# Second layer's MLP in two phases with down rows gated on GpSimd, and another order of loads at the start of the down phase

## The reference, cut to what matters

```python
def modulate(h, shift, scale):
    return layer_norm(h) * (1.0 + scale) + shift

def post_norm_residual(h, y, gate, g, b):
    return layer_norm_affine(DEEPNORM_ALPHA * h + gate * y, g, b)

def sq_relu_mlp(u, w1, w2):
    return jnp.square(jax.nn.relu(u @ w1)) @ w2
...
for i in range(DEPTH):                                  # DEPTH = 2; mlp0, mlp1
...
    h = post_norm_residual(h, sq_relu_mlp(modulate(h, sh2, sc2), mlp_w1[i], mlp_w2[i]), g2, ln_g[i, 1], ln_b[i, 1])
...
h = h + jnp.square(jax.nn.relu(_rmsnorm(h, mlp_norm_g[l]) @ w_up[l])) @ w_down[l]   # mlp2
```

## Time and profile before

| | us |
|---|---|
| three runs | 3166.06, 3170.08, 3171.18 |
| median | 3170.08 |
| the profiled execution | 3174.14 |
| its span, first to last instruction | 3172.4 |
| PE busy in it | 3061.9 |
| mean granted TensorE clock | 0.992 of full |

### The profile page before, as it was taken

The page is one execution under the profiler, slowest core; times in us unless marked ns, Lnnn a source line. Parts: engine busy times, 40 slices in busy tenths (PEclk is TensorE's granted clock), DMA queues, the critical chain, the costliest instruction groups (busy, mean ns, idle before and its releaser), DMA issues.

```text
span 3172.4 us, 36169 instructions
## 1 busy us (share of the span) xinstructions
PE 3061.9 (97%) x14331; PEld 2511.8 (79%) x14331; DVE 2130.2 (67%) x2769; ACT 1344.0 (42%) x2002; POOL 822.5 (26%) x543
## 2 busy tenths in 40 slices
PE   7999999999999999989999999999998999999998
PEld 2888888778888888868788888888777778887887
DVE  4716598577677777586766555666797676667576
ACT  4411387363333333442633333334427465553334
POOL 0010335155433443221444444314000212120000
PEclk9999999999999999999999999999999999999999
DMA  7426322212322332111111111121111225456533
GB/s 236 145 88 209 89 67 59 102 38 93 106 95 98 100 102 82 49 43 53 35 52 54 54 54 47 53 67 41 40 54 54 93 97 177 148 197 226 188 109 120
DMA packets 202163, 302.83 MB, mean 95 GB/s; under 512 B 12135, under 2 KB 137690, under 8 KB 201994
## 3 DMA queue, kind: packets, MB, share of 16 engines
q1 hardware_dynamic: 174906, 206.46, 20.7%
q0 software_dynamic: 18736, 63.65, 5.3%
q10 hardware_dynamic: 8352, 30.41, 2.7%
HBM read 251.19 MB, written 49.28 MB: 95 GB/s over the span
## 4 chain that ended last, share of the span: by engine, by line
PE 77%; DVE 12%; ACT 6%; issue 2%; DMA 2%; POOL 1%; SPq 0%; DVEq 0%; ACTq 0%; POOLq 0%
PE psum L669 24%; PE psum L671 23%; PE psum L670 23%; DVE page_r L680 2%; PE psum L1399 2%; DVE dw L4161 2%; DVE small L819 1%; ACT temp L1004 1%; ACT page_r L675 1%; ACT U_hi L675 1%; DVE U_lo L680 1%; DMA page<-in_ada_w_dram 1%; DVE H L1679 1%; PE psum L1374 1%; PE psum L865 1%
## 5 line engine op out<-in xcount | busy, mean ns | idle before, releaser
L669 PE MATMUL psum<-U_hi,page_r 128*128 128x512 f32 x1884 | 743.4, 395 | 24.6 <-DVE U_lo L680 9.7
L671 PE MATMUL psum<-U_hi,page_r 128*128 128x512 f32 x1884 | 734.7, 390 | 0.0
L670 PE MATMUL psum<-U_lo,page_r 128*128 128x512 f32 x1884 | 734.6, 390 | 0.0
L680 DVE TENSOR_TENSOR page_r<-page,page_r 128x1024 fp32r<-128x1024 f32 (+1 forms) x208 | 294.7, 1422 | 284.9 <-ACT page_r L675 276.2
L669 PE MATMUL psum<-page_r,act_page_r 128*128 128x512 f32 x1232 | 480.4, 390 | 5.6 <-DVE page_r L680 5.6
L670 PE MATMUL psum<-page_r,act_page_r 128*128 128x512 f32 x1232 | 480.1, 390 | 0.0
L669 PEld LDWEIGHTS psum<-U_hi,page_r 128*128 128x128 f32 x1884 | 354.3, 188 | 113.5 <-DVE U_lo L680 19.6
L671 PE MATMUL psum<-page_r,act_page_r 128*128 128x512 f32 x1120 | 436.4, 390 | 0.0
L675 ACT CAST page_r<-page 128x1024 fp32r<-128x1024 f32 (+1 forms) x271 | 276.3, 1024 | 324.5 <-DMA page<-in_mlp_w_dram 92.7
L671 PEld LDWEIGHTS psum<-U_hi,page_r 128*128 128x128 f32 x1884 | 354.2, 188 | 75.0
L670 PEld LDWEIGHTS psum<-U_lo,page_r 128*128 128x128 f32 x1884 | 354.6, 188 | 70.2
(11 more groups left out here) (394 smaller groups left out, 4809.8 us busy)
## 6 DMA issues: line engine op xcount, KB each, us to landing
page<-in_mlp_w_dram SPq DMA_DIRECT2D x128, 512.0 KB, 4.2
act_page<-d_act_mlp SPq DMA_DIRECT2D x56, 512.0 KB, 3.6
d_act_mlp<-page POOLq DMA_DIRECT2D x111, 256.0 KB, 5.8
page<-in_ada_w_dram SPq DMA_DIRECT2D x48, 512.0 KB, 4.7
page<-in_w_in_dram SPq DMA_DIRECT2D x38, 512.0 KB, 4.0
pair_raw<-in_w_up_dram SPq DMA_DIRECT2D x14, 1024.0 KB, 6.2
ada_land<-in_ada_w_dram ACTq DMA_DIRECT2D x24, 512.0 KB, 4.7
even_raw<-in_w_down_dram SPq DMA_DIRECT2D x8, 1024.0 KB, 6.2
```

Source lines behind the costliest of these rows:

```text
L669: pe.matmul(out, l_hi, r_hi, start=start, stop=False, skip_group_check=read_between)
L670: pe.matmul(out, l_hi, r_lo, start=False, stop=False, skip_group_check=read_between)
L671: return pe.matmul(out, l_lo, r_hi, start=False, stop=stop, skip_group_check=read_between)
L680: return dve.tensor_tensor(lo, src, hi.bitcast(F32), ALU.subtract).then_inc(*k.lo.inc(*key))
```

## The change

The second layer's MLP uses the two-phase functions too. What is new in them for it:

- POOL multiplies the down rows by the gate, 32 instructions of 128x2x512 (`pool_gate_rows`), in the order: two for product 1 before the last but one pair's spills, two more after the last pair's first spills, the rest behind all spills. ACT and DVE wait for the gated rows (`wait_rows`) where they waited for the loads.
- The first add of each quarter also multiplies H by ALPHA (one instruction as before).
- The boundary to the next stage is worked into the last two products: at step d of product 12 the post norm of tile d (measure, root, scale, normed tile; POOL's two operations follow), from (12, 2) on ACT's sums of squares for the pre-norm; the transposes of tiles 0 to 3 stand inside the last product on PE, between its second and third token tile, on four banks. Tiles 4 to 7 follow the last product's adds.
- The weight of the last step has a place of its own; other page slots and the loads of the next stage's weights move accordingly.

For both two-phase MLPs SP issues `acts(2)` and `acts(3)` ahead of `odds(0, 0)`.

```diff
-TWO_PHASE = ("mlp2",)
+TWO_PHASE = ("mlp1", "mlp2")
+GATE_OF = {"mlp1": (1, 1)}
...
+            if after and t == 1:
+                pe_turn_chunk(k, pe, on, after.name, 0, [after.place(k, e) for e in range(TPC)],
+                              lambda e: on.wait_ge(*after.hat(k, e)), slots=CHAIN_BANKS)
...
+def wait_rows(k, on, name, p, s, d):
+    if name in GATE_OF:
+        on.wait_ge(*k.pool_gated.at(name, p, s, d))
+    else:
+        on.wait_ge(*(k.odd_in if p in ("2", "3") else k.even_in)[d].at(name, s))
+
+def pool_gate_rows(k, pool, on, name, p, s, d):
+    rows = down_source(k, p, d)
+    cols = CH if p in ("7", "3") else 0
+    on.wait_ge(*k.gate_ok.at(*GATE_OF[name]))
+    on.wait_ge(*(k.odd_in if p in ("2", "3") else k.even_in)[d].at(name, s))
+    pool.tensor_tensor(rows, rows, k.row_gate[:, cols:cols + CH].unsqueeze(1).to_broadcast([P, 2, CH]), ALU.mult).then_inc(
+        *k.pool_gated.inc(name, p, s, d))
...
     if g == DOWN_STEPS - 1:
-        on.wait_ge(*k.lo.at("weight", name, g - 3))
+        on.wait_ge(*k.up_done.at(name, "4", PAIRS - 1))
...
         if p == "57":
-            on.wait_ge(*k.odd_in[e].at(name, s))
+            wait_rows(k, on, name, "7", s, e)
+            wait_rows(k, on, name, "3", s, e)
...
+def act_behind_step(k, act, on, b, i, d):
+    if i == FIRST_DONE + 1:
+        act_root(k, act, on, P, b.name, "post", d)
+        act_normed(k, act, on, b, d)
+    t = STEPS_OF * (i - FIRST_DONE - 1) + d - 2
+    if 0 <= t < TPC:
+        act_pre_square(k, act, on, b, t)
+
+def dve_behind_step(k, dve, on, b, i, d):
+    if i == FIRST_DONE + 1:
+        dve_norm_measure(k, dve, on, b, "post", d)
+        dve_norm_scale(k, dve, on, b, "post", d)
+        k.smalls.take(on, (b.name, "pre", d))
+    t = STEPS_OF * (i - FIRST_DONE - 1) + d - 3
+    if 0 <= t < TPC:
+        dve_norm_scale(k, dve, on, b, "pre", t)
...
+    gate("1", 0, 2)
+    gate("1", 0, 3)
     for what in ("12",) + sums:
         store(what, PAIRS - 1)
+    for d in range(STEPS_OF):
+        gate("7", 0, d)
+        gate("3", 0, d)
+    for d in range(STEPS_OF):
+        gate("2", 0, d)
+    for d in range(STEPS_OF):
+        gate("1", 1, d)
+        gate("7", 1, d)
+    for p in ("3", "2"):
+        for d in range(STEPS_OF):
+            gate(p, 1, d)
...
-    odds(0, 0)
     acts(2)
     acts(3)
+    odds(0, 0)
     odds(0, 1)
...
-    pe_mlp(k, pe, on, "mlp1", BOUNDARY[2], BOUNDARY[3])
+    pe_two_phase(k, pe, on, "mlp1", BOUNDARY[2], BOUNDARY[3])
```

More of the change, by code:

```diff
@@ L981, in dve_start, with pe_turn_chunk @@
         dve_weights(k, dve, on, s)
-def pe_turn_chunk(k, pe, on, stage, c, src, ready, groups=range(KT)):
+def pe_turn_chunk(k, pe, on, stage, c, src, ready, groups=range(KT), slots=(None,)):
     for i in groups:
-        b = k.banks.take(on, ("turn", stage, c, i), (k.taken, ("turn", stage, c, i)))
+        b = k.banks.take(on, ("turn", stage, c, i), (k.taken, ("turn", stage, c, i)), slot=slots[i % len(slots)])
         for t in range(TPC):
@@ L1015, in dve_turn_chunk @@
             between(i)
-STASHED = {"pre4": "mlp2"}
+STASHED = {"post2": "mlp1", "pre4": "mlp2"}
 def stash_of(k, c, i):
@@ L1785, in __init__, with behind @@
         self.on_pool = TT - 2 if from_u else TT - 1
+    @property
+    def behind(self):
+        return self.down[0] if self.down[0] in TWO_PHASE else None
     def by_pool(self, tt):
@@ L1818, in place_free @@
             on.wait_ge(*k.down_done.at(self.down, TT - 1, 1))
+        elif self.behind and tt < TPC:
+            on.wait_ge(*k.lo.at("weight", self.behind, STEPS_OF * (FIRST_DONE + 1) - 1))
+        elif self.behind and tt < TT - 2:
+            on.wait_ge(*k.up_done.at(self.behind, "4", PAIRS - 1))
+        elif self.behind:
+            on.wait_ge(*k.down_done.at(self.down, TT - 1, 1))
         elif not self.from_u:
@@ L1830, in u_free @@
             on.wait_ge(*k.down_done.at(self.down, TPC - 1 if c == 0 else TT - 1, 1))
+        elif self.behind and c == 0:
+            on.wait_ge(*k.lo.at("weight", self.behind, STEPS_OF * FIRST_DONE - 1))
+            on.wait_ge(*k.folded.at(self.behind, "down", 1, "6", STEPS_OF - 1))
+        elif self.behind:
+            on.wait_ge(*k.up_done.at(self.behind, "4", PAIRS - 1))
         else:
@@ L3010, in act_down_weight @@
     if p in ("1", "2", "3"):
[L3011 removed]
+        wait_rows(k, on, name, p, s, d)
     else:
@@ L3067, in dve_down_add, with act_pre_square, act_two_phase @@
         on.wait_ge(*k.h_back[tt].at(name))
-    dve.tensor_tensor(h, h, k.bank(name, "down", i, t), ALU.add).then_inc(*k.h_added.inc(name, i, t))
-    if DOWN_ORDER[i] in ("4", "2"):
+    if name in GATE_OF and not earlier:
+        m = dve.scalar_tensor_tensor(h, h, ALPHA, k.bank(name, "down", i, t), ALU.mult, ALU.add)
+    else:
+        m = dve.tensor_tensor(h, h, k.bank(name, "down", i, t), ALU.add)
+    m.then_inc(*k.h_added.inc(name, i, t))
+    if i >= len(PRODUCTS) and DOWN_ORDER[i] in ("4", "2"):
         k.h_added.also(name, tt)
+        k.h_added.also((name, BLOCKS - 1), tt, 1)
 FIRST_DONE = len(DOWN_ORDER) - 3
-def act_two_phase(k, act, on, name, before):
+def act_pre_square(k, act, on, b, t):
+    s = k.small[:, k.smalls.of(b.name, "pre", t), :]
+    on.wait_ge(*b.gained(k, t))
+    on.wait_ge(*k.act_done.now())
+    act.activation(k.ada_land[:], k.H[:, t, :], ACT.Square, scale=D ** -0.5, accum_out=s[:, 13:14]).then_inc(
+        *k.act_done.inc("pre", b.name, t))
+    on.wait_ge(*k.act_done.now())
+    act.activation(s[:, 14:15], s[:, 13:14], ACT.Sqrt, bias=k.eps[:, 0:1]).then_inc(*k.rooted.inc(b.name, "pre", t))
+def act_behind_step(k, act, on, b, i, d):
[13 more added lines that the diff above has]
+        dve_norm_scale(k, dve, on, b, "pre", t)
+def act_two_phase(k, act, on, name, before, after=None):
     row = lambda p, *part: act_row_sum(k, act, on, name, p, before, *part)
@@ L3092, in act_two_phase @@
             op("1", PLAIN + 1)
-        act_plain_tile(k, act, on, name, i, c)
+        if not (before.rows and (i, c) in UP_AHEAD):
+            act_plain_tile(k, act, on, name, i, c)
         if (i, c) == (FB - 1, 0):
```

91 lines of the change are left out of this document (64 added, 27 removed).

## The result

The changed kernel takes 3196.39 us (median of four, 3194.46 to 3197.54), the kernel before 3170.36 in the same comparison: 1.0082 of it, 95% interval 1.0069 to 1.0094. It is 26 us slower; 3174 was forecast, with a range from 3134 to 3188.

A forecast was written before the change was run, and what follows sets the result against it. PE's instruction count was taken to set the time, other engines mattering only where PE waits. Terms -43.4 - 3.6 - 4 + 23.2 + 6.4 + 22.2 + 3 gave +3.8 us, forecast 3174 us, range 3134 to 3188.

The forecast's parts named there:

- matmuls and old waits gone: mlp1: 192 fewer matmuls at 0.226 us, -43.4 us, and three waits of the merged last block gone, -3.6 us.
- start of the down phase: mlp1: 12 POOL gates behind the last spill alternate with DVE, so PE waits; +21 us, +2.2 for the lower clock.
- second half's gates: mlp1's down phase: 16 POOL gates beside DVE, partly absorbed; +6.4 us, ends 0 and 13, full alternation 8.
- product 12: mlp1: the norm's DVE-ACT chain and POOL's two operations per tile lengthen four steps; +20 us, full alternation 22.5.
- transposes: mlp1's last product: PE waits 1.6 to 4.4 us for ACT with four banks free; taken as +3 us.
- moved loads: mlp2's down phase: activations come about 2.8 us earlier, shortening the 5.61 us wait; -4 us, ends -1.5 to -7.8.
- the lower clock: mlp1: slower matmuls charged at 2.2 us each, behind the down phase start's longest wait and in product 12.
- (b): Rival, mlp1: DVE and POOL fully alternate wherever POOL has work; 3182 us, up to 3188; chance 0.22.
- (a): Rival, mlp1: gates slip into DVE's gaps; -31 us, or -29 with a clock drop, giving 3141; chance 0.28.
- Four fifths of the way: mlp1: share taken from gates in gaps (5 us) towards full alternation (25) at the down phase's start; also in product 12.
- PE's busy time should fall by 43 us: Sign, whole kernel: PE's busy time must fall by about 43 us.
- The other sign: mlp1: the prediction is wrong if the added waits are under 35 us or over 60.

The follow-up runs named there:

- e8: The changed kernel with 24 of the 32 gates done by DVE just ahead of the sums that read the rows; 3164.86 us, ratio 0.9982.
- e2: The changed kernel with POOL's two norm operations for tiles 0 to 3 at mlp1's end on 8 of 1024 columns; 3182.31 us, ratio 1.0035.
- e5: The changed kernel with the last product's eight groups of transposes spread behind its second, third and fourth token tiles; 3195.34 us, ratio 1.0081.
- e1: The changed kernel with each POOL gate on 2x8 of its 2x512 columns, same instructions, waits and loads; 3158.45 us, ratio 0.9961.
- e9: The changed kernel with each tile's norm in product 12 spread over two steps; 3188.42 us, ratio 1.0050.
- e12: The changed kernel with the edits of e8, e9 and e5, and DVE also doing the four gates of product 1's first half; 3156.63 us, ratio 0.9955.
- e4: The kernel before with only mlp2's loads moved, third and fourth step's activations ahead of the first odd rows; 3168.04 us, ratio 0.9993.
- e6: The changed kernel with the old order of loads, first odd rows ahead of those activations, in both two-phase MLPs; 3196.97 us, ratio 1.0086.

## Why the prediction was wrong, point by point

"Lower clock" is the time that is left when the waits and the matmuls at 0.2267 us each (the distance of two starts at full clock, a step is 5.44 us) are taken off a stretch between two rows.

| step of the sum | forecast | measured |
|---|---|---|
| matmuls and old waits gone | -47.0 | -47.1 (by count) |
| mlp1's up phase: new waits, old ones gone, lower clock | 0 | +6.6, -2.1, +1.9 |
| start of the down phase (to step 6), with lower clock | +23.2 | +25.0 |
| second half's gates, with lower clock | +6.4 | +13.5 |
| product 12 | +20 | +20.4 |
| last product: transposes, with lower clock | +5.2 | +8.9 |
| moved loads in mlp2 and all else behind mlp1 | -4 | -1.6 |
| ahead of mlp1 (scatter) | 0 | -3.3 |
| sum | +3.8 | +22.2 (span +22.3) |

(The 5.2 are the 3 for the transposes and the 2.2 for the clock behind product 12.)

The mechanism, DVE and POOL alternating on a shared port, was right; the terms were too small. Three failed. The second half's gates, taken at +6.4, cost 13.5. The up phase of mlp1 stood at nothing, with no reason given, and cost 6.4. And the lower clock was charged behind two waits, 4.4 us, while it followed on nearly all: where no later wait took it up, about 13 us.

- **Matmuls**: right. PE's busy time fell by 20 us less than by count; the lower clock, at which matmuls take longer, accounts for it. In the down phase, from 1853.9 to 2230.7, 1344 matmuls and the transposes are worth 308.9 us and the waits 48.8; 19 of the 376.8 us are left for the lower clock. I had put in 4.4. It followed on nearly all waits of over 2 us, down to one of 2.40 us (from 1973.87 to 2058.92 are 14 steps of 5.44, the wait of 6.55, and 2.3 more). The earlier trace rows had shown it behind a wait of 5.61. But not all of the 19 us came on top: some 8 of them, in product 12 and behind the first wait of the down phase, lie between waits for engines that set the round, where PE would have waited longer at the full clock (see e8). That leaves about 11 in the down phase, and 1.9 in the up phase.
- **Start of the down phase**: right in size (25 by full alternation, 21 + 2.2 taken, 25.0 measured, of which waits are 20.7), wrong in its shape in the profiled execution: I had the first wait at the fourth step, and POOL's long hold of the port brought it to the third. In e2 and e5 the waits are 4.9, 5.9 and 5.8 and 4.8, 4.7 and 6.2 us, before the third, fourth and fifth step, where I had 10, 8.5 and 5.5 before the fourth, fifth and sixth; with the lower clock e2's start costs some 23 us. That the whole came out near is in part luck. e1 shows the cause: without the gates' time 4.1 us are left, against the 5 that I gave to loads alone. e8 shows that it is POOL's hold and not the multiplication.
- **Second half's gates**: the mechanism was right (e1: both waits gone), the size too small: 13.5 against 6.4, my upper end of 13 nearly to the point. I had taken four fifths of full alternation's 8; here the waits are the full price, 8.95, and the lower clock behind them, which I had put at nothing, is 4.6 on top.
- **Product 12**: right, 20.4 against 20; a round takes 10.35 us where full alternation would give 10.8. The 20.4 are 14.3 of waits and 6.1 of lower clock; as the other engines set the round, it is their sum that the 20 stood for, and the four fifths that gave it had no row behind them: the hit is in part luck. e2 and e9 show both parts of it, POOL's operations (11.3 us of e2's gain lie in product 12; its start was some 2.4 better) and the chain between DVE and ACT.
- **Transposes**: the waits between groups are 4.6 us, beyond my 4.4, and the clock adds 4.3.
- **What was not in the sum**: the up phase. The 3.75 us come from ACT, busy with the sums of rows when PE wants a bank; mlp2 had no such wait in the trace of before, and I expected none in mlp1 either. The 1.65 and 1.23 are two early gates beside DVE; I had said that they only come before the last spills (e1: both gone; e12: one gone, one 0.76). Small waits of 4.4 us at mlp1's start stood in the trace of before, where I had read none; 2.1 of them went. **Moved loads**: -1.4 us of wait in mlp2, -2.7 in e4, near the smaller of my ends, and by e5 and e6 not clear of scatter.
- **Rivals**: (b), full alternation, named place and price (3182 to 3188; its own ends add up to 3189) and is the case that came, 8 us beyond its end, by the lower clock and the up phase. (a) is out by e1: what slipped into gaps in mlp1's blocks doesn't at a start with twelve gates in a row. "Four fifths of the way" rested on a median of gates in another stretch; the rows of alternation bore on this place, the median did not. With 0.35 on slower, the range should have gone to (b) with all ends added: waits of 25, 13 and 22.5, and the clock behind each wait that no later one takes up.
- **What I said would show it**: PE's busy time should fall by 43 us and fell by 22.7, a sign that struck. The other sign, added waits in mlp1 under 35 or over 60 us, did not: its waits grew by 50 (from 8.4 to 58.3). A sign that counts waits alone misses the lower clock.

## What to carry to other kernels

Work moved to GpSimd isn't free when VectorE has two-input operations on the critical path beside it: add up the time of both engines on the port over the stretch in which it runs (here 2.4 us for a gate on POOL, 1.14 on DVE) and compare it with that stretch, not with the busy share of the whole. Where PE has nothing queued, charge a wait also with the matmuls that then run at the lower clock, unless another wait for the same slow engines follows at once and takes that time up: here 19 us went with 49 us of waits, and some 11 of them came on top. Two engines that hand a small result back and forth in the middle of a step should do it a step apart.
